# Scores of the later queries in steps of two chunks, with the keys' residues multiplied on 64 rows, in a two-block transformer kernel

## The chip, the cores and the metric

The kernel runs on one core of a Trainium2 chip. The metric is the device time of one launch in microseconds (us), from start to end; lower is better. TensorE (PE) multiplies matrices, VectorE (DVE), ScalarE (ACT) and GpSimd (POOL) do element-wise work, SyncE (SP) issues transfers. Each engine runs its own instructions in the order written; semaphores tie them together.

## What is computed

Two blocks over 1024 tokens of width 1024, in float32: first gated linear attention, a short convolution and a gated feed-forward layer; then spatial gating beside dilated attention. The change lies in the dilated attention alone (and in how GpSimd makes one residue). Cut to what matters:

```python
N_HEADS, HEAD_DIM, BLOCK = 16, 64, 128
DILATED_PATTERNS = ((128, 1), (512, 4), (2048, 16))

def dilated_pattern(q, k, v, slopes, window, dilation):
    ...
    s = jnp.einsum('bhrnqd,bhrnkd->bhrnqk', qb, kw) * (Dh ** -0.5)
    s = s - slopes[...] * (dist * dilation)
    s = jnp.where(valid[None, None, None], s, NEG_INF)
    m = jnp.max(s, axis=-1)
    p = jnp.exp(s - m[..., None])
    l = jnp.sum(p, axis=-1)
    o = jnp.einsum('bhrnqk,bhrnkd->bhrnqd', p, vw) / l[..., None]
    return o, m, l

def dilated_attention(q, k, v):
    outs = [dilated_pattern(qh, kh, vh, slopes, w, d) for (w, d) in DILATED_PATTERNS]
    m_all = max over the patterns of m
    alphas = [l * jnp.exp(m - m_all) for (_, m, l) in outs]
    return sum(a * o) / sum(alphas)
```

The kernel computes the three patterns at once: one dense causal score row per query, to which the penalty on the distance and the logarithm of the number of patterns that hold a key are added (a very negative number where there is none).

## The kernel before

**Split operands.** Every large product is made of three fast products. A float32 operand x becomes x_hi (a value rounded to the fast format) and the residue x_lo = x - x_hi, and W·x is W_hi·x_hi + W_hi·x_lo + W_lo·x_hi (L791 to L793). W_hi is made by ScalarE (L1185), W_lo by GpSimd in `split` (L686), one instruction of 1024 columns for each unit. A unit is one tile of 128 output columns of a weight: two halves of 512 tokens by 8 tiles of depth, that is 16 groups of three matmuls.

**Attention in stages.** Heads go in pairs; a pair has four units of projections (gates) left over from the input projection, and each of them is one *stage*: TensorE runs the unit's 16 groups of three dense matmuls, and behind each group stands a small piece of attention work. There are 32 stages (8 pairs by 4). Stage m of a pair scores head m // 2; with m even the early queries (tokens 0 to 511, an *even stage*), with m odd the later queries (512 to 1023, an *odd stage*), and beside it the softmax rows of the stage before are turned and multiplied with V. Which step stands behind which group is a string for each parity and engine: `PE_STEPS`, where a slash separates the groups, `ACT_STEPS` and `DVE_STEPS`, which are plain sequences. A step is skipped where it doesn't apply. The letters, with the lines:

- PE: s = scores of one chunk of keys (`score_chunk`, L1094 and L1095), t = four or fewer transposes of the softmax rows of the stage before (L1110), o = those with V (L1122, L1123), v = transposes of V (L1075, at the end of stage 0 of a pair only).
- ACT: e = exp of a query block (L1595), p = the fast part of a transposed chunk (L1605), w = W_hi of the next unit (L1185), a = a gate's tanh (L1618), q, k = the fast parts of the next head's queries and keys (L1460, L1464), O = half of the output (L1609), v = V's fast part (L1659), d, y = stores.
- DVE: r = scores plus bias with the running minimum (L2215), n = reciprocal and normalisation of a query block (L2225, L2227), l = residue of a transposed chunk (L2234), z = copy of the unit before out of PSUM (L2198), m = a gate's product (L2250), b = bias table of the next head (L2091, 1024 columns), q, k = residues of queries and keys (L2096, L2101), O = output (L2242), v = V's residue (L2281).

**Scores.** A head has 64 columns, and `att_q_split` uses all 128 rows: rows 0 to 63 hold q_hi and rows 64 to 127 hold q_lo, against the same keys loaded twice. One matmul with `att_k_hi` gives (q_hi + q_lo)·k_hi, a second with `att_k_lo` gives (q_hi + q_lo)·k_lo, into the same bank. An odd stage has four query blocks with two chunks of keys each: 512 and 128, 512 and 256, 512 and 384, 512 and 512 columns. They take turns in banks 2 and 0, and chunk n waits until DVE has taken chunk n - 2 (the semaphore `ttr`, L1090). Even stages have four chunks (128, 256, 384, 512), all in bank 2.

**What ties a stage to the next.** t0 of a stage waits for all four n of the stage before (`pn`, L1104), o waits for its l (`pl`, L1117), e for its block's last r, p for its t, l for its p, n for its e.

Of the kernel before, what the change touches and what calls it, by code (L numbers as in the profile page):

```python
# [25 lines left out]
P = 128  # L26
D = 1024
S = 1024
# [7 lines left out]
HEADS, DH = 16, 64  # L36
# [129 lines left out]
def steps_before(m):  # L166

    return 12 * (m // 2) + 4 * (m % 2)

def chunks_of(m):
# [16 lines left out]

PE_STEPS = [
    "t0/t1//o0 t2/s0/o1 t3/s1/o2 t4/s2/o3 t5/s3/o4 t6//o5 t7/o6/o7 v0 v1",  # L190
    "s0//s1/s2/t0/s3/s4/s5 o0 t1//s6/s7 o1 t2///o2 t3//o3",
]
PE_STEPS = [x.split("/") for x in PE_STEPS]
ACT_STEPS = [
# [2 lines left out]
]  # L197
DVE_STEPS = [
    "O l0 k l1 z l2 r0 l3 r1 n0 l4 r2 n1 l5 r3 n2 l6 m n3 l7",
    "v0 r0 v1 O r1 r2 z n0 l0 r3 r4 n1 l1 r5 m r6 r7 l2 n2 b l3 n3 q",  # L200
]

PE_REST = "t0 t1//o0 t2//o1 t3//o2 t4//o3 t5//o4 t6//o5 t7//o6//o7//".split("/")
# [26 lines left out]
def two_blocks(nc, xT, weights, vecs, gate_up, mix_w, mix_b, dist, logm, ident, out):  # L230
    f32, f32r = mybir.dt.float32, mybir.dt.float32r
    ALU = mybir.AluOpType
# [3 lines left out]
    with ctx:  # L236

        at = {}
# [45 lines left out]
        K2 = place("att_k", S, f32, xr + 4096)  # L284
        VT = place("att_v", S, f32, xr + 8192)
        QS = place("att_q_split", S, f32r, xr + 12288)
        KH = place("att_k_hi", S, f32r, xr + 16384)
        KL = place("att_k_lo", S, f32r, xr + 20480)
        VHL = place("att_v_split", [2, NBLK, P], f32r, xr + 24576)
# [393 lines left out]
        def _(pool):  # L683
            def split(u):
                pool.wait_ge(w_hi, u.count(1))
                pool.tensor_tensor(WL[:, u.slot], WR[:, u.slot], WH[:, u.slot].bitcast(f32),  # L686
                                   ALU.subtract).then_inc(w_lo, 1)

            def splits(c, n):
                if n >= 2:  # L690
# [79 lines left out]
        def _(pe):  # L770
# [308 lines left out]
            def score_chunk(pair, m, n):  # L1079

                i, c, w = chunks_of(m)[n]
                base, sb = steps_before(m), m % 2
                bank = 0 if sb and n % 2 else 2
                if n == 0 and sb == 0:
                    pe.wait_ge(q_lo, pair.count(2, m // 2 + 1))
                    pe.wait_ge(k_lo, pair.count(2, m // 2 + 1))
                if m == 1 and n == 1:
                    pe.wait_ge(v_lo, pair.count(2, 1))
                if n >= 1 + sb:
                    pe.wait_ge(ttr, pair.count(24, base + n - sb))  # L1090
                elif sb and n == 0:
                    pe.wait_ge(ttr, pair.count(24, base))
                dst = PA[:, bank, 0:w]
                pe.matmul(dst, QS[:, i * P:(i + 1) * P], KH[:, c:c + w], start=True, stop=False)  # L1094
                pe.matmul(dst, QS[:, i * P:(i + 1) * P], KL[:, c:c + w], start=False, stop=True  # L1095
                          ).then_inc(s_ready, 1)

            def turn_p(pair, m, k):

# [26 lines left out]
            def stage(pair, m, before=None, **have):  # L1126
                def between(g):
                    for kind, n in steps(PE_STEPS[m % 2][g], before=bool(before), first=m == 0):
                        if kind == "s":
                            score_chunk(pair, m, n)  # L1130
                        elif kind == "t":
                            turn_p(*before, n)
                        elif kind == "o":
                            weigh_v(*before, n)
                        else:
                            v_transposes(pair, n)
# [40 lines left out]
        def _(act):  # L1177
# [279 lines left out]

            def head_q(pair, h):
                act.wait_ge(q_in, pair.count(64, 32 * h + 32))
                act.activation(QS[:], Q2[:], ACT.Copy, scale=DH ** -0.5).then_inc(q_hi, 1)  # L1460

            def head_k(pair, h):
                act.wait_ge(k_in, pair.count(64, 32 * h + 32))
# [265 lines left out]
        def _(dve):  # L1729
# [363 lines left out]

            def head_q(pair, h):
                dve.wait_ge(q_hi, pair.count(2, h + 1))
                dve.scalar_tensor_tensor(QS[DH:P], Q2[DH:P], DH ** -0.5, QS[DH:P].bitcast(f32),  # L2096
                                         ALU.mult, ALU.subtract).then_inc(q_lo, 1)

            def head_k(pair, h):
# [323 lines left out]
```

## Time and profile before

| | us |
|---|---|
| three runs | 2412.66, 2410.06, 2413.32 |
| median | 2412.66 |
| profiled execution, its own time | 2410.62 |
| its span, first to last instruction | 2408.9 |
| TensorE busy in the span | 2351.6 |
| VectorE, ScalarE, GpSimd busy | 1345.0, 861.6, 736.6 |
| mean granted TensorE clock, share of full | 0.994 |

The span is 1.7 us shorter than the execution's own time. Rows name the line, the engine, the operation, the tiles (written <- read) and the shape; a time in brackets is how long the engine sat idle before, and who ended that. The end of a matmul is modelled, so its pace is read from starts: dense matmuls of 512 columns start 0.23 us apart although each is shown as 0.39 us long.

### The profile page before, as it was taken

Reading aid. Unit: us, or ns where it says so; the run is one execution under the profiler, and the core shown is the slowest. Engines: PE = TensorE matmul, PEld = TensorE weight load, DVE = VectorE, ACT = ScalarE, POOL = GpSimd, SP = SyncE. Lnnn points to the kernel's source line nnn. Section 1 sums busy time; section 2 is a strip of 40 time slices with the busy share of each in tenths; the row PEclk is TensorE's granted clock in tenths of the full one; section 3 lists DMA queues with packets and bytes.
Section 4 is the critical chain, followed back from the end, with each engine's and each line's share of the span. In section 5 each row is a group of like instructions: output and inputs, shape, how many; then the busy total and the mean of one; then the engine's idle time right before and its main releaser. Section 6 shows DMA issues by size and latency. Waiting matters only on the chain.

```text
span 2408.9 us, 29740 instructions
## 1 busy us (share of the span) xinstructions
PE 2351.6 (98%) x11076; PEld 1938.9 (80%) x11076; DVE 1345.0 (56%) x1790; ACT 861.6 (36%) x1293; POOL 736.6 (31%) x416
## 2 busy tenths in 40 slices
PE   9999999999999999999999999999999999999997
PEld 6888788878888888888888888778787787778886
DVE  4444763754444443347653444777877778753444
ACT  4422222242333331143343223555545555441122
POOL 2121221264555522222455555211122112212221
PEclk9999999999999999999999999999999999999998
DMA  3111222232222243233312223523233232353223
GB/s 133 44 44 35 88 79 96 86 144 85 79 79 80 84 169 105 70 114 114 118 53 83 101 95 111 178 76 113 78 113 106 77 113 78 105 181 124 105 96 113
DMA packets 69168, 237.94 MB, mean 99 GB/s; under 512 B 8241, under 2 KB 10449, under 8 KB 68945
## 3 DMA queue, kind: packets, MB, share of 16 engines
q1 hardware_dynamic: 53568, 181.53, 22.2%
q10 hardware_dynamic: 15504, 55.10, 5.7%
q8 instruction: 65, 1.06, 0.2%
q14 instruction: 31, 0.25, 0.0%
HBM read 177.35 MB, written 59.24 MB: 98 GB/s over the span
## 4 chain that ended last, share of the span: by engine, by line
PE 93%; DVE 4%; issue 1%; DMA 1%; ACT 1%; SPq 0%; DVEq 0%; ACTq 0%
PE dense L791 18%; PE dense L792 18%; PE dense L793 18%; PE dense L974 9%; PE dense L975 9%; PE dense L976 9%; PE aux L1110 3%; PE aux L1094 2%; PE aux L1095 1%; PE aux L1123 1%; PE aux L1122 1%; PE aux L1057 1%; DVE att_p_lo L2234 1%; DVE x_lo L1964 1%; PE aux L821 0%
## 5 line engine op out<-in xcount | busy, mean ns | idle before, releaser
L686 POOL TENSOR_TENSOR w_lo<-w_raw,w_hi 128x1024 fp32r<-128x1024 f32 x123 | 303.3, 2466 | 1097.0 <-ACT w_hi L1185 1087.9
L791 PE MATMUL dense<-x_hi,w_hi 128*128 128x512 f32 x1456 | 596.7, 410 | 5.8 <-DVE x_lo L1736 2.1
L792 PE MATMUL dense<-x_lo,w_hi 128*128 128x512 f32 x1456 | 570.7, 392 | 0.0
L793 PE MATMUL dense<-x_hi,w_lo 128*128 128x512 f32 x1456 | 570.7, 392 | 0.0
L1185 ACT CAST w_hi<-w_raw 128x1024 fp32r<-128x1024 f32 x121 | 127.1, 1050 | 555.7 <-PE dense L793 548.8
L793 PEld LDWEIGHTS dense<-x_hi,w_lo 128*128 128x128 f32 x1456 | 274.8, 189 | 59.8
L791 PEld LDWEIGHTS dense<-x_hi,w_hi 128*128 128x128 f32 x1456 | 275.5, 189 | 56.6 <-issue 8.6
L792 PEld LDWEIGHTS dense<-x_lo,w_hi 128*128 128x128 f32 x1456 | 276.1, 190 | 46.6 <-issue 1.9
L721 POOL TENSOR_TENSOR w_lo<-w_sums,w_hi 128x512 fp32r<-128x512 f32 x144 | 228.3, 1594 | 240.9 <-ACT w_hi L1341 240.9
L974 PE MATMUL dense<-x_hi,w_hi 128*128 128x512 f32 x576 | 226.1, 392 | 0.0
L976 PE MATMUL dense<-x_hi,w_lo 128*128 128x512 f32 x576 | 224.2, 389 | 0.0
L975 PE MATMUL dense<-x_lo,w_hi 128*128 128x512 f32 x576 | 224.2, 389 | 0.0
L1341 ACT CAST w_hi<-w_sums 128x512 fp32r<-128x512 f32 x144 | 89.2, 620 | 242.8 <-DVE w_sums L1973 176.1
L974 PE MATMUL dense<-x_sums_split,w_hi 128*128 128x512 f32 x432 | 168.4, 390 | 2.4 <-DVE work L2180 1.2
L976 PE MATMUL dense<-x_sums_split,w_lo 128*128 128x512 f32 x432 | 168.2, 389 | 0.0
L975 PE MATMUL dense<-x_sums_split,w_hi 128*128 128x512 f32 x432 | 168.1, 389 | 0.0
L1605 ACT CAST att_p_hi<-aux 128x512 fp32r<-128x512 f32 x192 | 92.2, 480 | 145.9 <-PE aux L1110 145.5
L2234 DVE TENSOR_TENSOR att_p_lo<-aux,att_p_hi 128x512 fp32r<-128x512 f32 x192 | 106.3, 554 | 60.3 <-ACT att_p_hi L1605 58.0
L791 PE MATMUL dense<-work_split,w_hi 128*128 128x512 f32 x352 | 137.0, 389 | 1.5 <-DVE work L2049 1.5
L793 PE MATMUL dense<-work_split,w_lo 128*128 128x512 f32 x352 | 136.9, 389 | 0.0
L792 PE MATMUL dense<-work_split,w_hi 128*128 128x512 f32 x352 | 136.9, 389 | 0.0
L974 PEld LDWEIGHTS dense<-x_hi,w_hi 128*128 128x128 f32 x576 | 108.2, 188 | 23.0 <-issue 1.0
(270 smaller groups left out, 3815.7 us busy)
## 6 DMA issues: line engine op xcount, KB each, us to landing
w_raw<-weights SPq DMA_DIRECT2D x163, 512.0 KB, 4.1
w_raw_b<-weights SPq DMA_DIRECT2D x34, 512.0 KB, 4.3
kept_qkv<-work ACTq DMA_DIRECT2D x24, 512.0 KB, 2.7
kept_m<-work ACTq DMA_DIRECT2D x22, 512.0 KB, 2.6
work<-kept_m SPq DMA_DIRECT2D x22, 512.0 KB, 3.3
residual<-xT SPq DMA_DIRECT2D x16, 512.0 KB, 7.1
kept_x<-residual ACTq DMA_DIRECT2D x16, 512.0 KB, 2.6
att_q<-kept_qkv SPq DMA_DIRECT2D x32, 256.0 KB, 3.9
```

Source lines behind the costliest of these rows:

```text
L686: pool.tensor_tensor(WL[:, u.slot], WR[:, u.slot], WH[:, u.slot].bitcast(f32), ALU.subtract).then_inc(w_lo, 1)
L721: pool.tensor_tensor(WL[:, h // 2, at4], quarter(p, i), WH[:, h // 2, at4].bitcast(f32), ALU.subtract).then_inc(*((d_lo, 1) if i < 6 else ...
L791: pe.matmul(dst, WH[:, u.slot, k], hi, start=(k == 0), stop=False)
L792: pe.matmul(dst, WH[:, u.slot, k], lo, start=False, stop=False)
L793: last = pe.matmul(dst, WL[:, u.slot, k], hi, start=False, stop=(k == nk - 1))
L974: pe.matmul(bank(b), wh, hi[:, j], start=(first and j == 0), stop=False, skip_group_check=True)
L975: pe.matmul(bank(b), wh, lo[:, j], start=False, stop=False, skip_group_check=True)
L976: last = pe.matmul(bank(b), wl, hi[:, j], start=False, stop=(j == 3), skip_group_check=True)
L1185: act.copy(WH[:, u.slot], WR[:, u.slot]).then_inc(w_hi, 1)
L1341: act.copy(WH[:, h // 2, 4 * (h % 2):4 * (h % 2) + 4], quarter(p, i)).then_inc(*((d_hi, 1) if i < 6 else (w_hi, 2)))
L1605: act.copy(PH[:, k % 2, lo:HALF], PA[:, bank, lo:HALF]).then_inc(ph, 1)
L2234: dve.tensor_tensor(PL[:, k % 2, lo:HALF], PA[:, bank, lo:HALF], PH[:, k % 2, lo:HALF].bitcast(f32), ALU.subtract).then_inc(pl, 1)
```

## The change

The strings of the odd stages on PE and DVE are new. On PE the eight s are replaced by four x, each for the two chunks of one query block (`score_chunks`); x waits until DVE has taken all chunks before it. x first multiplies both chunks with `att_k_hi` on 128 rows. Then it multiplies `att_k_lo` on 64 rows only, rows 0 to 63 for the first chunk and rows 64 to 127 for the second, with a new tile `att_q_hi_twice` that holds q_hi in both halves. The term q_lo·k_lo is left out in odd stages. ScalarE's q makes `att_q_hi_twice` (128 rows) and then rows 0 to 63 of `att_q_split`: two instructions of 1024 columns where one was. GpSimd's `split` becomes two instructions of 512 columns with one semaphore increment behind the second. Even stages keep their strings and `score_chunk`.

```diff
 PE_STEPS = [
     "t0/t1//o0 t2/s0/o1 t3/s1/o2 t4/s2/o3 t5/s3/o4 t6//o5 t7/o6/o7 v0 v1",
-    "s0//s1/s2/t0/s3/s4/s5 o0 t1//s6/s7 o1 t2///o2 t3//o3",
+    "//x0/t0//x1/o0 t1//x2/o1 t2//x3/o2 t3///o3",
 ]
 DVE_STEPS = [
     "O l0 k l1 z l2 r0 l3 r1 n0 l4 r2 n1 l5 r3 n2 l6 m n3 l7",
-    "v0 r0 v1 O r1 r2 z n0 l0 r3 r4 n1 l1 r5 m r6 r7 l2 n2 b l3 n3 q",
+    "v0 v1 O r0 r1 z l0 r2 r3 n0 l1 r4 r5 n1 l2 m r6 r7 n2 l3 b n3 q",
 ]
@@ def split (GpSimd)
-                pool.tensor_tensor(WL[:, u.slot], WR[:, u.slot], WH[:, u.slot].bitcast(f32),
-                                   ALU.subtract).then_inc(w_lo, 1)
+                for at4 in (slice(0, 4), slice(4, 8)):
+                    last = pool.tensor_tensor(WL[:, u.slot, at4], WR[:, u.slot, at4],
+                                              WH[:, u.slot, at4].bitcast(f32), ALU.subtract)
+                last.then_inc(w_lo, 1)
@@ new on TensorE
+            def score_chunks(pair, m, n):
+
+                pe.wait_ge(ttr, pair.count(24, steps_before(m) + 2 * n))
+                if m == 1 and n == 0:
+                    pe.wait_ge(v_lo, pair.count(2, 1))
+                both = chunks_of(m)[2 * n:2 * n + 2]
+                for (i, c, w), bank in zip(both, (2, 0)):
+                    pe.matmul(PA[:, bank, 0:w], QS[:, i * P:(i + 1) * P], KH[:, c:c + w], start=True, stop=False)
+                for (i, c, w), bank, rows in zip(both, (2, 0), (slice(0, DH), slice(DH, P))):
+                    pe.matmul(PA[:, bank, 0:w], QHH[rows, i * P:(i + 1) * P], KL[rows, c:c + w],
+                              start=False, stop=True).then_inc(s_ready, 1)
@@ head_q on ScalarE
-                act.activation(QS[:], Q2[:], ACT.Copy, scale=DH ** -0.5).then_inc(q_hi, 1)
+                act.activation(QHH[:], Q2[:], ACT.Copy, scale=DH ** -0.5)
+                act.activation(QS[0:DH], Q2[0:DH], ACT.Copy, scale=DH ** -0.5).then_inc(q_hi, 1)
@@ head_q on VectorE
-                dve.scalar_tensor_tensor(QS[DH:P], Q2[DH:P], DH ** -0.5, QS[DH:P].bitcast(f32),
+                dve.scalar_tensor_tensor(QS[DH:P], Q2[DH:P], DH ** -0.5, QHH[DH:P].bitcast(f32),
                                          ALU.mult, ALU.subtract).then_inc(q_lo, 1)
```

TensorE, the third query block of an odd stage. Before, its two chunks stand alone, behind groups 6 and 7 (the second is the one shown, with what follows it):

```order
L792 MATMUL dense<-x_lo,w_hi 128x512
L793 MATMUL dense<-x_hi,w_lo 128x512
L1090 REGISTER_ALU
L1094 MATMUL aux<-att_k_hi,att_q_split 128x384
L1095 MATMUL aux<-att_k_lo,att_q_split 128x384
L1119 REGISTER_ALU
L1122 MATMUL aux<-att_p_hi,att_v_split 128x512
```

Now both chunks stand behind group 8 as one x (the shape shown is that of the output):

```order
L795 MATMUL dense<-x_lo,w_hi 128x512
L796 MATMUL dense<-x_hi,w_lo 128x512
L1099 REGISTER_ALU
L1104 MATMUL aux<-att_k_hi,att_q_split 128x512
L1104 MATMUL aux<-att_k_hi,att_q_split 128x384
L1106 MATMUL aux<-att_k_lo,att_q_hi_twice 128x512
L1106 MATMUL aux<-att_k_lo,att_q_hi_twice 128x384
L794 MATMUL dense<-x_hi,w_hi 128x512
```

The last two chunks stood behind groups 9 and 10; their x3 stands behind group 11.

VectorE, from the middle of an odd stage. Before, n0 (L2227 on 640 columns) and l0 stand between the copy z and the third and fourth r:

```order
L2198 COPY work<-dense 128x1024
L2224 REGISTER_ALU
L2225 RECIPROCAL softmax_stats<-softmax_stats 128x1
L2227 TENSOR_SCALAR att_p_late<-att_p_late,softmax_stats 128x640
L2234 TENSOR_TENSOR att_p_lo<-aux,att_p_hi 128x512
L2212 REGISTER_ALU
L2215 ISA att_p_late,softmax_stats<-aux,att_bias,softmax_stats 128x256
```

Now the r of a block's two chunks stand together, and n0 behind the second block's:

```order
L2212 COPY work<-dense 128x1024
L2248 TENSOR_TENSOR att_p_lo<-aux,att_p_hi 128x512
L2226 REGISTER_ALU
L2229 ISA att_p_late,softmax_stats<-aux,att_bias 128x512
L2229 ISA softmax_stats 128x1
L2226 REGISTER_ALU
L2229 ISA att_p_late,softmax_stats<-aux,att_bias,softmax_stats 128x256
L2229 ISA softmax_stats 128x1
L2238 REGISTER_ALU
L2239 RECIPROCAL softmax_stats<-softmax_stats 128x1
L2241 TENSOR_SCALAR att_p_late<-att_p_late,softmax_stats 128x640
```

VectorE, the end of an odd stage. Before, the bias table b stands ahead of l3:

```order
L2227 TENSOR_SCALAR att_p_late<-att_p_late,softmax_stats 128x896
L2091 ISA
L2091 SCALAR_TENSOR_TENSOR att_bias<-distances,vectors,log_counts 128x1024
L2234 TENSOR_TENSOR att_p_lo<-aux,att_p_hi 128x128
L2224 REGISTER_ALU
L2225 RECIPROCAL softmax_stats<-softmax_stats 128x1
L2227 TENSOR_SCALAR att_p_late<-att_p_late,softmax_stats 128x1024
```

Now it stands behind l3 and ahead of n3:

```order
L2241 TENSOR_SCALAR att_p_late<-att_p_late,softmax_stats 128x896
L2248 TENSOR_TENSOR att_p_lo<-aux,att_p_hi 128x128
L2105 ISA
L2105 SCALAR_TENSOR_TENSOR att_bias<-distances,vectors,log_counts 128x1024
L2238 REGISTER_ALU
L2239 RECIPROCAL softmax_stats<-softmax_stats 128x1
L2241 TENSOR_SCALAR att_p_late<-att_p_late,softmax_stats 128x1024
```

## Rows read from the trace of the kernel before

**Rows 1.** The page, part 1: busy us, share of the span, instructions.

```profile
PE 2351.6 (98%) x11076; PEld 1938.9 (80%) x11076; DVE 1345.0 (56%) x1790; ACT 861.6 (36%) x1293; POOL 736.6 (31%) x416
```

**Rows 2.** Waits: engine, line, whom it waited for, us in total, times, longest.

```profile
PE aux L1094 <- DVE softmax_stats L2215: 25.1, 16, 1.9
```

**Rows 3.** Timeline (start, length in us), TensorE, the wait in two odd stages.

```profile
1807.44 0.39 PE L793 MATMUL dense<-x_hi,w_lo 128*128 128x512 f32 x1
1809.06 0.44 PE L1094 MATMUL aux<-att_k_hi,att_q_split 128*128 128x384 f32 x1 [1.23 <-DVE softmax_stats L2215]
1809.34 0.34 PE L1095 MATMUL aux<-att_k_lo,att_q_split 128*128 128x384 f32 x1
...
1844.66 0.39 PE L793 MATMUL dense<-x_hi,w_lo 128*128 128x512 f32 x1
1846.96 0.44 PE L1094 MATMUL aux<-att_k_hi,att_q_split 128*128 128x384 f32 x1 [1.91 <-DVE softmax_stats L2215]
```

**Rows 4.** Timeline ahead of the first wait, three engines; a half-length GpSimd residue elsewhere.

```profile
1806.07 1.93 DVE L2227 TENSOR_SCALAR att_p_late<-att_p_late,softmax_stats 128x640 f32<-128x640 f32 x1
1808.53 0.47 DVE L2215 CUSTOM_DVE_ANT_0 att_p_late<-aux,att_bias,softmax_stats 128x256 f32<-128x256 f32 x1
...
1805.26 2.39 POOL L686 TENSOR_TENSOR w_lo<-w_raw,w_hi 128x1024 fp32r<-128x1024 f32 x1 [16.91 <-ACT w_hi L1185]
...
1804.16 1.03 ACT L1185 CAST w_hi<-w_raw 128x1024 fp32r<-128x1024 f32 x1
...
1512.50 1.29 POOL L721 TENSOR_TENSOR w_lo<-w_sums,w_hi 128x512 fp32r<-128x512 f32 x1 [1.98 <-ACT w_hi L1341]
```

**Rows 5.** Timeline, TensorE: a run of 64-row matmuls, then part of it alone.

```profile
173.07 0.39 PE L793 MATMUL dense<-x_hi,w_lo 128*128 128x512 f32 x1
173.38 2.06 PE L918 MATMUL aux<-work 64*128 64x128 f32 x32
...
175.71 0.39 PE L792 MATMUL dense<-x_lo,w_hi 128*128 128x512 f32 x1
...
173.71 1.40 PE L918 MATMUL aux<-work 64*128 64x128 f32 x22
```

**Rows 6.** Timeline, TensorE: 32-row matmuls of 512 columns, then part of them alone.

```profile
56.54 0.39 PE L793 MATMUL dense<-x_hi,w_lo 128*128 128x512 f32 x1
...
60.82 0.39 PE L792 MATMUL dense<-x_lo,w_hi 128*128 128x512 f32 x1
...
57.39 2.30 PE L872 MATMUL aux<-work,gate_up_w 32*128 32x512 f32 x5
```

**Rows 7.** Timeline, TensorE: a chunk of 128 columns between dense matmuls.

```profile
1802.41 0.22 PE L1094 MATMUL aux<-att_k_hi,att_q_split 128*128 128x128 f32 x1
...
1802.87 0.39 PE L792 MATMUL dense<-x_lo,w_hi 128*128 128x512 f32 x1
```

**Rows 8.** Timeline, an odd stage's end: TensorE's last score, VectorE, ScalarE, TensorE.

```profile
1813.08 0.39 PE L1095 MATMUL aux<-att_k_lo,att_q_split 128*128 128x512 f32 x1
...
1813.66 0.75 DVE L2215 CUSTOM_DVE_ANT_0 att_p_late<-aux,att_bias,softmax_stats 128x512 f32<-128x512 f32 x1 [0.45 <-PE aux L1095]
...
1815.60 1.28 DVE L2091 SCALAR_TENSOR_TENSOR att_bias<-distances,vectors,log_counts 128x1024 f32<-128x1024 f32 x1
1816.80 0.28 DVE L2234 TENSOR_TENSOR att_p_lo<-aux,att_p_hi 128x128 fp32r<-128x128 f32 x1
...
1817.19 0.75 DVE L2227 TENSOR_SCALAR att_p_late<-att_p_late,softmax_stats 128x1024 f32<-128x1024 f32 x1
...
1814.45 1.15 ACT L1595 ACTIVATE att_p_late<-att_p_late,softmax_stats 128x1024 f32<-128x1024 f32 x1
...
1816.49 0.27 ACT L1605 CAST att_p_hi<-aux 128x128 fp32r<-128x128 f32 x1 [0.80 <-PE aux L1110]
...
1818.60 0.60 PE L1110 MATMUL aux<-identity,att_p_late 128*128 128x128 f32 x4
```

**Rows 9.** Window, length, busy us by engine, then granted clock: another such wait.

```profile
1764.00:1776.00 12.00, 10.10 (x43) 8.08 (x43) 9.96 (x20) 5.74 (x9) 4.74 (x2) 0.86 0.01 5
```

More of the change, by code:

```diff
@@ L286, in two_blocks @@
         QS = place("att_q_split", S, f32r, xr + 12288)
+        QHH = place("att_q_hi_twice", S, f32r, at["rstd"])
         KH = place("att_k_hi", S, f32r, xr + 16384)
@@ L1082, in score_chunk @@
                 base, sb = steps_before(m), m % 2
-                bank = 0 if sb and n % 2 else 2
-                if n == 0 and sb == 0:
+                bank = 2
+                if n == 0:
                     pe.wait_ge(q_lo, pair.count(2, m // 2 + 1))
                     pe.wait_ge(k_lo, pair.count(2, m // 2 + 1))
[L1087 to L1092, printed above, removed]
+                if n >= 1:
+                    pe.wait_ge(ttr, pair.count(24, base + n))
                 dst = PA[:, bank, 0:w]
@@ L1130, in between @@
                             score_chunk(pair, m, n)
+                        elif kind == "x":
+                            score_chunks(pair, m, n)
                         elif kind == "t":
```

## The prediction

> **What bounds the kernel now.** I read the page first: TensorE is busy 98% of the span [rows 1], so time goes only where TensorE does less work or waits less. Then the waits of TensorE: in the attention stages there is one large group, 16 waits of L1094 for VectorE's r, 25.1 us of idle time [rows 2]. Sixteen is one for each odd stage. The timeline shows what one costs: dense matmuls start 0.23 us apart, here L793 starts at 1807.44 and the next matmul at 1809.06, 1.39 us late, and L1095 follows 0.28 us behind instead of 0.17 (its weights were not loaded ahead), so 1.50 us. The stages with m = 1 lose more: 1844.66 to 1846.96 is 2.07 us late, 2.18 with the same 0.11 [rows 3]. Eight of each make 29.4 us. The cause is ahead of it on VectorE: n0 takes 1.93 us on 640 columns, while GpSimd's residue runs from 1805.26 to 1807.65, and r3, for which TensorE waits, starts only behind it [rows 4]; n3 on 1024 columns takes 0.75 [rows 8]. This is the wait that the change goes for.
>
> **TensorE's work in an x.** Two 64-row matmuls on different rows run as one: 22 of L918 with 128 columns take 1.40 us, the last of them started 0.27 before the end, so a pair takes 0.112 us [rows 5], while the same type of matmul with 512 columns takes 0.43 [rows 6], or 0.107 for 128: two for one. I use that for the residues. It saves the second chunk's L1095. A chunk of 128 columns cost 0.23 us for its two matmuls (1802.41 to 1802.87 less 0.23 for L791) [rows 7], and one narrow full-row matmul in the new place costs its width, 0.06: 0.17 saved. In the same way 256 saves 0.12, 384 saves 0.17, 512 saves 0.23. Together 0.70 us for an odd stage.
>
> But going from full rows to fewer and back is not free. From L793 at 173.07 to L792 at 175.71 are 2.64 us. Less 0.23 for L793, 0.23 for L791 and 16 pairs by 0.112, 0.39 remain for the way in and out [rows 5]. The 32-row run gives the same with 512 columns: 60.82 less 56.54 is 4.28, less 0.46 for two dense and 8 by 0.43, 0.40 [rows 6]. Bounds for one x: 0 (the chip could load the 64-row weights ahead here) and 0.40; I take 0.40, as both rows give it. Four x an odd stage are 1.6 less 0.70, **+0.88 us an odd stage, +14.1 us for 16.**
>
> **The old wait.** It goes. r0 to r5 now stand ahead of what needs them, x1 to x3 are three groups (2.05 us) and more apart, and VectorE's two r last at most 0.69 and 0.75 [rows 8]. n0 stands behind r3, and GpSimd's two halves of 1.29 [rows 4] follow the cast w. Whether VectorE slips in between them no longer matters to TensorE. The halves cost GpSimd 0.2 us a unit, behind which nothing waits: w_lo is due a whole unit (18 us) later. -29.4 us.
>
> The Trainium skill (SBUF — State Buffer, Terms) says that VectorE and GpSimd share a port pair under an exclusive lock, held for a full instruction; n0's 1.93 us [rows 4] agrees, and a half-length instruction would by it hold VectorE up half as long.
>
> **What is late next.** I lay the new order out from the start of an odd stage, a group of three dense matmuls at 0.68 us.
> First, o0. x0 stands behind three groups: its residues start at 2.54, r0 starts 0.58 after them (the latency of 1813.08 to 1813.66 [rows 8]), r0 and r1 end at 4.1, since both are now needed for e0. Then ScalarE's e0 (0.83), w (1.03 [rows 4]) and p0 (0.59), the two others by the width of e3 [rows 8], VectorE's l0 (0.69), and o0 can start at 7.3. TensorE comes to it at 7.14 (seven groups, x0, t0, x1). A wait of 0.2, and 0.11 for weights not loaded ahead: 0.31.
> Second, the end. x3 stands behind group 11, where the last two chunks stood behind groups 9 and 10. The chain from the start of x3 to the next stage's t0, in which each step needs the one before: full-row matmuls 0.46, the switch 0.20, 0.58 to r6, r6 0.62, r7 0.75, e3 1.19, p3 0.27, l3 0.31, then b, which now stands between l3 and n3, 1.21, the reciprocal 0.20, n3 0.75, the semaphore 0.06 [rows 8]; 6.60, and 6.49 with VectorE's instructions overlapping by 0.07 here and there. TensorE has between the same points: x3 1.09, five groups 3.41, o2, t3 and o3 0.61: 5.1. So it is 1.4 us early in all, of which 0.2 to 0.3 pass at o3 for l3 and the rest at t0 for n3, and with the 0.11 behind t0 it loses 1.5. Before, r7 had begun 0.58 behind a score that came 1.2 us earlier in the stage, and b ran in an idle gap ahead of l3: n3 ended at 1817.94, t0 started at 1818.60 [rows 8], 0.66 us to spare. In stages with m = 1 the gate product m stands ahead of r6 and makes it 0.5 us later: 2.0.
> Waits after: 0.31 + 1.5 in eight stages and 0.31 + 2.0 in eight, 33 us; the last odd stage has no b, -1.2: **31.7 us against 29.4 before, +2.3.**
>
> The extra instruction in ScalarE's q (about 1.1 us, e3's length for as many columns [rows 8]) stands at the end of an odd stage. Behind it are O, p0 and k, then VectorE's k, for which s0 waits; laid out in the same way, k is done 1.1 us before s0 is due, so it costs nothing, and up to 1 us a stage if that cover is gone. Dropped q_lo·k_lo costs nothing.
>
> **Clock.** In 1764 to 1776, around one such wait, the granted clock was 0.86 of full [rows 9], that is, a part of it at 1.2 GHz. The waits that follow one another at o3 and t0 are about as long, so I leave this as it is; two such windows go or come at some 1.7 us each.
>
> **Sum.** 2410.6 (the profiled execution) + 14.1 - 29.4 + 31.7 = 2427.0. The median lies 2 us above that execution; half of this added gives **2428 us, 0.6% slower**.
>
> **Rivals.**
> 1. *Faster: n3 comes in time.* Place: the chain from x3 to t0. It decides at 1.4 us: if that chain is 5.1 us or less instead of 6.5, there is no wait at the end, and only o0's 0.31 is left, 4.9 us in all. The time would be 2410.6 + 14.1 - 29.4 + 4.9 = 2400, and 2397 with the two slow-clock windows gone. For it: TensorE had 0.66 us to spare [rows 8]. Against it: each length in the chain is a row, and b alone takes 1.28 of VectorE. Chance 0.13.
> 2. *The switch is free.* Then TensorE has 25 us less work, but it comes sooner to o0 and o3, where the chains over ScalarE are as long as before. Laid out anew, o0 waits 0.6 us longer and o3 0.2 to 0.6, so only about 10 us come back: 2418. Against it are both rows of the switch. Chance 0.12.
> 3. *The residues run one after another*, so that the change doesn't do what it says. 0.58 us more work an odd stage, almost all inside the waits for o0 and o3, which shrink by as much: 2430. Rows 5 speak against it. Chance 0.06.
> 4. *More waits:* k or the first score of an even stage is late by some 0.5 us, and slow-clock windows behind the waits: 2438. Chance 0.08.
> 5. *The end's wait is half of what I think* (0.7 us a stage): 2417. Chance 0.09.
> My forecast has 0.52.
>
> **How the numbers follow.** A measurement of this kernel tells 0.2% (4.8 us) from no change: 2407.8 to 2417.5 is the same. Faster is rival 1, 0.13. Same are halves of rivals 2 and 5, 0.11. The rest is slower, 0.76. The range leaves out rival 1 and the upper half of rival 4: 2410 to 2437.
>
> **What would show it.** L1094's wait for VectorE in odd stages gone; in its place waits of L1110 (t0) and of the last L1122 in odd stages for VectorE, near 1.1 us 15 times and 0.2 to 0.7 us 16 times; n0 near 0.6 to 1.1 us instead of 1.93 and more. Starts 0.2 us apart more than the width before and behind each pair of 64-row matmuls, the two of a pair starting together. Odd stages as long as now, even stages 1.2 us longer. I am wrong if t0 starts straight behind its group, or if the matmul behind an x starts 0.23 us after the residues.

## The result, and the profile after

| | before | after |
|---|---|---|
| median | 2412.99 us (2410.06 to 2414.69, 4 runs) | 2439.9 us (2435.22 to 2440.96, 4 runs) |
| after over before | | 1.0109, 95% interval 1.0092 to 1.0127 |
| profiled execution, its own time | 2410.62 | 2440.96 |
| its span | 2408.9 | 2439.2 |
| mean granted clock | 0.994 | 0.993 |

The change costs 27 us, 1.1%. The forecast was 15 us, with a range that ended at 2437.

The page of the profile after, part 1, answers [rows 1]: TensorE works 25 us longer, VectorE 48 us less.

```profile
PE 2376.4 (97%) x11076; PEld 1927.4 (79%) x11076; DVE 1296.8 (53%) x1790; ACT 870.7 (36%) x1309; POOL 794.8 (33%) x539
```

The waits of TensorE for VectorE in the attention stages. The one of [rows 2] is gone, and two stand in its place, 32 at o and 16 at t0 (the end of a matmul is modelled, so these totals are too small; below I read the lateness from starts):

```profile
PE aux L1133 <- DVE att_p_lo L2248: 20.2, 32, 1.2
PE aux L1121 <- DVE att_p_late L2241: 10.6, 16, 0.9
```

The timeline of TensorE in one odd stage (m = 3), from x0 to o0, with one group in between left out:

```profile
1816.38 0.39 PE L796 MATMUL dense<-x_hi,w_lo 128*128 128x512 f32 x1
1816.61 0.45 PE L1104 MATMUL aux<-att_k_hi,att_q_split 128*128 128x512 f32 x2
1816.99 0.50 PE L1106 MATMUL aux<-att_k_lo,att_q_hi_twice 64*128 64x512 f32 x2
1817.42 0.50 PE L794 MATMUL dense<-x_hi,w_hi 128*128 128x512 f32 x1
1817.76 0.40 PE L795 MATMUL dense<-x_lo,w_hi 128*128 128x512 f32 x1
...
1821.48 0.40 PE L796 MATMUL dense<-x_hi,w_lo 128*128 128x512 f32 x1
1822.37 0.50 PE L1133 MATMUL aux<-att_p_hi,att_v_split 128*128 128x512 f32 x1 [0.50 <-DVE att_p_lo L2248]
...
1828.33 0.62 PE L1104 MATMUL aux<-att_k_hi,att_q_split 128*128 128x512 f32 x2
1828.88 0.50 PE L1106 MATMUL aux<-att_k_lo,att_q_hi_twice 64*128 64x512 f32 x2
1829.31 0.50 PE L794 MATMUL dense<-x_hi,w_hi 128*128 128x512 f32 x1
```

A row with x2 holds both chunks. The two residues of x0 (512 and 128 columns) take 0.43 us to the next start, and so do the two of x3 (512 and 512): the narrower one costs nothing beside the wider. That is the two for one of [rows 5]. The way in and out is in the same rows: from x0 at 1816.61 to L795 at 1817.76 are 1.15 us, less 0.23 for L794, less 0.29 for 640 full-row columns, less 0.23 for the residues, leaves 0.40 us. The same sum for x3, with L795 0.34 behind L794, is 1.32 - 0.23 - 0.46 - 0.23 = 0.40.

o0 should have followed L796 at 1821.71 and starts at 1822.37, 0.66 us late. The same view at the end of this stage, then at the end of a stage with m = 1:

```profile
1832.31 0.40 PE L796 MATMUL dense<-x_hi,w_lo 128*128 128x512 f32 x1
1833.11 0.33 PE L1133 MATMUL aux<-att_p_hi,att_v_split 128*128 128x128 f32 x1 [0.40 <-DVE att_p_lo L2248]
...
1833.89 0.39 PE L796 MATMUL dense<-x_hi,w_lo 128*128 128x512 f32 x1
1835.16 0.66 PE L1121 MATMUL aux<-identity,att_p_late 128*128 128x128 f32 x4 [0.88 <-DVE att_p_late L2241]
...
1871.49 0.40 PE L796 MATMUL dense<-x_hi,w_lo 128*128 128x512 f32 x1
1873.07 0.33 PE L1133 MATMUL aux<-att_p_hi,att_v_split 128*128 128x128 f32 x1 [1.19 <-DVE att_p_lo L2248]
...
1874.31 0.39 PE L796 MATMUL dense<-x_hi,w_lo 128*128 128x512 f32 x1
1875.13 0.66 PE L1121 MATMUL aux<-identity,att_p_late 128*128 128x128 f32 x4 [0.43 <-DVE att_p_late L2241]
```

Here o3 is 0.57 us late and t0 1.04; with m = 1 they are 1.35 and 0.59 late. Each wait costs about another 0.11 behind it: from o0 to the next start are 0.34 us (1822.37 to 1822.71) instead of 0.23, as in the prediction. So a stage loses 0.77 at o0, and 1.83 (m = 3) or 2.16 (m = 1) at its end: 16 by 0.77, 8 by 1.83 and 8 by 2.16 are 44 us, where the forecast had 31.7.

VectorE in the same stage: the two r of x0, then of x3, and what follows up to n3, for which t0 waits; then ScalarE's three steps ahead of o0.

```profile
1817.68 0.69 DVE L2229 CUSTOM_DVE_ANT_0 att_p_late<-aux,att_bias 128x512 f32<-128x512 f32 x1 [1.67 <-PE aux L1106]
1818.29 0.08 DVE L2229 DVE_READ_ACCUMULATOR2_ANT softmax_stats<- 128x1 f32 x1
1818.65 0.35 DVE L2229 CUSTOM_DVE_ANT_0 att_p_late<-aux,att_bias,softmax_stats 128x128 f32<-128x128 f32 x1 [0.28 <-DVE softmax_stats L2229]
...
1829.57 0.69 DVE L2229 CUSTOM_DVE_ANT_0 att_p_late<-aux,att_bias 128x512 f32<-128x512 f32 x1 [0.26 <-PE aux L1106]
...
1830.54 0.75 DVE L2229 CUSTOM_DVE_ANT_0 att_p_late<-aux,att_bias,softmax_stats 128x512 f32<-128x512 f32 x1 [0.28 <-DVE softmax_stats L2229]
...
1832.97 1.28 DVE L2105 SCALAR_TENSOR_TENSOR att_bias<-distances,vectors,log_counts 128x1024 f32<-128x1024 f32 x1
...
1834.35 0.75 DVE L2241 TENSOR_SCALAR att_p_late<-att_p_late,softmax_stats 128x1024 f32<-128x1024 f32 x1
```

```profile
1819.05 0.83 ACT L1609 ACTIVATE att_p_late<-att_p_late,softmax_stats 128x640 f32<-128x640 f32 x1 [3.76 <-DVE softmax_stats L2229]
...
1819.87 1.03 ACT L1198 CAST w_hi<-w_raw 128x1024 fp32r<-128x1024 f32 x1
1820.93 0.59 ACT L1619 CAST att_p_hi<-aux 128x512 fp32r<-128x512 f32 x1
```

The second r starts 0.97 us after the first, and VectorE sits idle for 0.28 of it, released by its own earlier result. The chain was laid out with 0.62.

The group of instructions that held up TensorE before, n0, is short now (columns: busy us, mean ns of one): 554 ns each, against 1.93 us in [rows 4].

```profile
L2241 DVE TENSOR_SCALAR att_p_late<-att_p_late,softmax_stats 128x640 f32<-128x640 f32 x16 | 8.9, 554 | 0.6
```

The lengths of the stages, from the last dense matmul of one unit to that of the next, read from the starts in the timelines; sums are over the four stages of a pair:

| us | m = 2 | m = 3 | m = 0 | m = 1 | sum |
|---|---|---|---|---|---|
| before | 19.04 | 17.99 | 18.36 | 19.53 | 74.92 |
| after | 20.90 | 18.20 | 20.12 | 19.07 | 78.29 |

The row "before" is one pair; its stages with m = 2 scatter from 18.4 to 19.0 us (the reason stands under e7_switch_alone). Eight pairs by 3.37 us are 27 us, all of the difference of the medians; over all stages but the first the difference is 26.8 us. (The profiled executions differ by 30 us; the rest lies outside the attention.) Both traces have two stages in the attention with a stretch at a lower granted clock, so the clock is no part of it; the window that answers [rows 9]:

```profile
1716.00:1728.00 12.00, 11.56 (x57) 9.43 (x56) 8.86 (x17) 6.15 (x11) 2.53 (x2) 0.86 0.64 171
```

### The profile page after: what moved, and what is told of

Same layout as the page of the kernel before. It is cut to its first block, busy times and chain, and to the rows that moved or that the text cites. A ratio compares the mean times of both kernels' runs of the same rounds, so it can differ in the third digit from the quotient of the medians.

```text
span 2439.2 us, 29866 instructions
## 1 busy us (share of the span) xinstructions
PE 2376.4 (97%) x11076; PEld 1927.4 (79%) x11076; DVE 1296.8 (53%) x1790; ACT 870.7 (36%) x1309; POOL 794.8 (33%) x539
## 4 chain that ended last, share of the span: by engine, by line
PE 84%; DVE 6%; issue 4%; ACT 2%; POOL 1%; DMA 1%; ACTq 0%; DVEq 0%; SPq 0%; POOLq 0%
PE dense L794 16%; PE dense L796 16%; PE dense L795 16%; PE dense L977 8%; PE dense L979 8%; PE dense L978 8%; PE aux L1121 2%; PE aux L1133 1%; PE aux L1134 1%; DVE att_p_late L2229 1%; POOL att_mixed L754 1%; DVE att_bias L2105 1%; PE aux L1106 1%; DVE att_p_lo L2248 1%; ACT w_hi L1198 1%
## 5 line engine op out<-in xcount | busy, mean ns | idle before, releaser
L688 POOL TENSOR_TENSOR w_lo<-w_raw,w_hi 128x512 fp32r<-128x512 f32 x246 | 366.1, 1509 | 1068.1 <-ACT w_hi L1198 1058.9
L794 PE MATMUL dense<-x_hi,w_hi 128*128 128x512 f32 x1456 | 603.6, 415 | 5.5 <-POOL w_lo L688 2.1
L796 PE MATMUL dense<-x_hi,w_lo 128*128 128x512 f32 x1456 | 572.2, 393 | 0.0
L795 PE MATMUL dense<-x_lo,w_hi 128*128 128x512 f32 x1456 | 571.4, 392 | 0.0
L794 PEld LDWEIGHTS dense<-x_hi,w_hi 128*128 128x128 f32 x1456 | 275.7, 189 | 70.9 <-issue 23.2
L796 PEld LDWEIGHTS dense<-x_hi,w_lo 128*128 128x128 f32 x1456 | 275.0, 189 | 59.8
L795 PEld LDWEIGHTS dense<-x_lo,w_hi 128*128 128x128 f32 x1456 | 276.5, 190 | 45.9 <-issue 2.0
L794 PE MATMUL dense<-work_split,w_hi 128*128 128x512 f32 x352 | 137.1, 390 | 1.7 <-DVE work L2063 1.7
L796 PE MATMUL dense<-work_split,w_lo 128*128 128x512 f32 x352 | 137.0, 389 | 0.0
L795 PE MATMUL dense<-work_split,w_hi 128*128 128x512 f32 x352 | 137.0, 389 | 0.0
L1951 DVE TENSOR_TENSOR residual<-dense,residual 128x1024 f32<-128x1024 f32 x32 | 39.2, 1225 | 169.3 <-PE dense L796 169.3
```

The source lines that it names most:

```text
L688: last = pool.tensor_tensor(WL[:, u.slot, at4], WR[:, u.slot, at4], WH[:, u.slot, at4].bitcast(f32), ALU.subtract)
L794: pe.matmul(dst, WH[:, u.slot, k], hi, start=(k == 0), stop=False)
L795: pe.matmul(dst, WH[:, u.slot, k], lo, start=False, stop=False)
L796: last = pe.matmul(dst, WL[:, u.slot, k], hi, start=False, stop=(k == nk - 1))
```

## The experiments

The first theory was that of the forecast, with one correction: r behind r costs 0.97 us instead of 0.62, because the second waits for the first one's result, and this stands twice on TensorE's path in an odd stage (ahead of o0, and ahead of t0). Its rivals were that the end's chain was misread (b, the residues' latency), that the 64-row matmuls cost more than 0.40, and that GpSimd's halves hold something up. The kernels take the change apart from both sides: parts of it added to the kernel before, and parts of it undone in the changed kernel.

### What the old wait was worth: halves and order apart

e1_halves is the kernel before with GpSimd's residue in halves only.

```diff
-                pool.tensor_tensor(WL[:, u.slot], WR[:, u.slot], WH[:, u.slot].bitcast(f32),
-                                   ALU.subtract).then_inc(w_lo, 1)
+                for at4 in (slice(0, 4), slice(4, 8)):
+                    last = pool.tensor_tensor(WL[:, u.slot, at4], WR[:, u.slot, at4],
+                                              WH[:, u.slot, at4].bitcast(f32), ALU.subtract)
+                last.then_inc(w_lo, 1)
```

> The kernel before with GpSimd's residue in two instructions of 512 columns and nothing else. Theory A (the waits come from the order on VectorE and from what holds n0 up): n0 is held up only until the end of the first half, some 1.1 us less, in all 16 odd stages; L1094 waits 0.4 to 0.9 us instead of 1.5 to 2.2: 2413 - 18 = 2395 us. Rival (VectorE doesn't get in between the halves): n0 as long as before, 2413 us, or 1 us more.

Measured: 2394.53 us, ratio 0.9925 (0.9908 to 0.9941). All 16 waits are shorter. The view shows only the eight with m = 1; those with m = 3 have fallen below what it counts, but by the starts they are still 0.28 us late, and their stages (16.87 us) are 0.37 longer than without any wait (16.50, next run), those with m = 1 (18.43) 1.07:

```profile
PE aux L1096 <- DVE softmax_stats L2217: 6.1, 8, 0.8
```

n0 takes 1.15 us on average here instead of 2.27, which fits the reading that a second instruction of 512 columns gives VectorE an opening in the middle.

e2_halves_n0_later has the halves, and n0 behind the fifth r (r4):

```diff
-    "v0 r0 v1 O r1 r2 z n0 l0 r3 r4 n1 l1 r5 m r6 r7 l2 n2 b l3 n3 q",
+    "v0 r0 v1 O r1 r2 z l0 r3 r4 n0 n1 l1 r5 m r6 r7 l2 n2 b l3 n3 q",
```

> As e1_halves, and in the odd stages' order on VectorE n0 stands behind the third and fourth r (... z l0 r3 r4 n0 n1 ...); TensorE's steps are those of before. Theory A: no wait of TensorE is left in odd stages: 2413 - 28 = 2385 us. Rival (what is late next comes at once, at o0 or o3): 2395 us or more.

Measured: 2380.69 us, ratio 0.9865 (0.9849 to 0.9882). TensorE has no wait for VectorE left in an odd stage. Stages: 18.99, 16.50, 18.34, 17.36.

e6_n0_later has only that string; GpSimd's residue is whole, as before.

> The kernel before with only the order on VectorE of e2_halves_n0_later; GpSimd's residue in one piece. Theory A (the wait is made by what stands behind n0): TensorE doesn't wait in odd stages, as in e2: 2381 to 2383 us. Rival (the halves are needed as well): 2390 us or more.

Measured: 2380.67 us, ratio 0.9876 (0.986 to 0.9893), and the same stages within 0.03 us. So once n0 is out of the way of r3, the halves are worth nothing, and the string alone brings 31 us. Against before, a stage with m = 3 is 1.49 us shorter and one with m = 1 2.17, where the forecast read 1.50 and 2.18 for the old wait, 29.4 us in all. The two stretches at a lower clock, some 1.6 us each, are gone as well.

e9_whole_residue is the mirror: the changed kernel with GpSimd's residue in one instruction again (the diff of e1_halves the other way round).

> The changed kernel with GpSimd's residue in one piece as before. In the new order n0 stands behind r3 and starts 2.7 us after GpSimd in the stages with m = 3, so it is held up for little of it. Forecast's view (the halves do nothing once n0 stands later): 2440 us, within 3 us. Rival (VectorE's other instructions with two operands are held up too): 2445 us or more.

Measured: 2440.48 us, ratio 1.0114 (1.0097 to 1.0132), as the changed kernel. The halves neither help nor harm there. The forecast had them at nothing.

### The switch by itself

e7_switch_alone is e2_halves_n0_later with the residue of each second chunk on 64 rows, without a partner:

```diff
-                pe.matmul(dst, QS[:, i * P:(i + 1) * P], KL[:, c:c + w], start=False, stop=True
+                rows = slice(0, DH) if sb and n % 2 else slice(0, P)
+                pe.matmul(dst, QS[rows, i * P:(i + 1) * P], KL[rows, c:c + w], start=False, stop=True
```

> As e2_halves_n0_later (no waits of TensorE in the attention stages), but in odd stages the residue product of each second chunk (four a stage, 64 in all) is multiplied on rows 0 to 63 of att_q_split alone, which leaves out q_lo times k_lo there; nothing is paired. It measures the switch of rows by itself. Forecast's value, 0.40 us each: 2381 + 25 = 2406 us. Rival (free): 2381 us. Rival (half hidden): 2393 us.

Measured: 2403.53 us (10 runs), 22.8 us over e2_halves_n0_later, or 0.36 us for each of the 64. The odd stages are longer by 1.50 and 1.51 us, four by 0.375; the stage with m = 2 is shorter by 0.42. That is a hold of TensorE at its start, which e2_halves_n0_later has in six of eight such stages and e7_switch_alone in none: from the last dense matmul of m = 1 over o3 to the first of the next unit are 1.01 us (from 1838.30) in the one and 0.56 (from 1849.74) in the other:

```profile
1839.31 0.49 PE L793 MATMUL dense<-x_hi,w_hi 128*128 128x512 f32 x1 [0.23 <-issue]
```

```profile
1850.30 0.49 PE L793 MATMUL dense<-x_hi,w_hi 128*128 128x512 f32 x1
```

No release that the profile shows ends it, and its cause stays open. Four of the eight stages with m = 2 before have it and six in the changed kernel, so it is hardly part of what the change costs. The price of a switch is therefore read from the odd stages. TensorE around one such residue of 384 columns:

```profile
1803.45 0.34 PE L1096 MATMUL aux<-att_k_hi,att_q_split 128*128 128x384 f32 x1
1803.72 0.44 PE L1098 MATMUL aux<-att_k_lo,att_q_split 64*128 64x384 f32 x1
1804.08 0.50 PE L1125 MATMUL aux<-att_p_hi,att_v_split 128*128 128x512 f32 x1
1804.42 0.40 PE L1126 MATMUL aux<-att_p_lo,att_v_split 128*128 128x512 f32 x1
```

By widths these three intervals would be 0.17, 0.17 and 0.23; they are 0.27, 0.36 and 0.34, that is 0.10, 0.19 and 0.11 more, 0.40 together. The Trainium skill (TensorEngine Tiling (Array Packing), Key Properties) says that a change of mode drains TensorE and gives no price; these rows agree, and the price here is 0.36 to 0.40 us for the way in and out together.

e3_full_rows is the changed kernel with the residues on all 128 rows, in the same steps of two chunks:

```diff
-                for (i, c, w), bank, rows in zip(both, (2, 0), (slice(0, DH), slice(DH, P))):
-                    pe.matmul(PA[:, bank, 0:w], QHH[rows, i * P:(i + 1) * P], KL[rows, c:c + w],
+                for (i, c, w), bank in zip(both, (2, 0)):
+                    pe.matmul(PA[:, bank, 0:w], QS[:, i * P:(i + 1) * P], KL[:, c:c + w],
                               start=False, stop=True).then_inc(s_ready, 1)
```

> The changed kernel, steps of two chunks and all orders kept, but the keys' residues are multiplied on 128 rows with att_q_split as before. Takes away the switch of rows (0.40 us an x as forecast) and adds back 0.58 us of matmuls an odd stage: 1.0 us less work an odd stage. Theory A: TensorE then comes sooner to o0 and o3 and waits there; half is eaten: 2440 - 8 = 2432 us. Rival B (the loss is mostly the switch): 2440 - 16 = 2424 us or less. Rival C (the switch costs nothing and only the pairing saved): 2449 us.

Measured: 2438.84 us, ratio 1.0106 (1.0089 to 1.0123). The expectation missed, by 7 us. The work did become less: stages of m = 3, 0 and 1 are 17.64, 20.11 and 18.53, and those of m = 2 22.35 with, 21.15 without a stretch at a lower clock. Without such stretches a pair is 0.86 us shorter than in the changed kernel, 6.9 us in all, near the 8 of theory A; o0 is 1.02 us late instead of 0.66, so TensorE waits for part of what it saves. The clock takes the rest back. The mean granted clock is 0.988 instead of 0.993, and seven of the stages with m = 2 have a stretch at a lower clock, where the changed kernel has two. Windows of the same place, the changed kernel first, then e3_full_rows (columns: length, busy us of PE, PEld, DVE, ACT, POOL, granted clock):

```profile
1792.00:1804.00 12.00, 10.15 (x53) 7.78 (x53) 10.60 (x17) 7.96 (x13) 4.45 (x3) 1.00 0.40 132
```

```profile
1790.00:1802.00 12.00, 10.12 (x44) 7.60 (x44) 10.99 (x19) 7.53 (x11) 4.41 (x3) 0.86 0.35 120
```

0.86 over 12 us means that a part of them ran at 1.2 GHz and the rest at 2.4. Such a stage is some 1.2 us longer here and 1.4 to 1.5 in the changed kernel, so seven against two take back nearly 6 of the 6.9 us. What TensorE did before the fall is the wait ahead of it: o3 starts 1.6 us late in these stages, 1.35 us in the changed kernel.

```profile
1793.03 0.33 PE L1133 MATMUL aux<-att_p_hi,att_v_split 128*128 128x128 f32 x1 [1.43 <-DVE att_p_lo L2248]
```

That wait does not decide it: the last stage with m = 2 has the same 1.6 us and no fall. Why there are five more falls stays open. The number of them changes from one trace to the next with edits that have nothing to do with it (two in e5_r_apart, three in e9_whole_residue, four in e10_own_wait_second).

### The end's chain, and r behind r

e4_b_last is the changed kernel with b behind n3:

```diff
-    "v0 v1 O r0 r1 z l0 r2 r3 n0 l1 r4 r5 n1 l2 m r6 r7 n2 l3 b n3 q",
+    "v0 v1 O r0 r1 z l0 r2 r3 n0 l1 r4 r5 n1 l2 m r6 r7 n2 l3 n3 b q",
```

> The changed kernel with the bias table b behind n3 instead of ahead of it (... l3 n3 b q). Theory A: t0 of even stages no longer waits for n3 (1.0 and 0.6 us), o0 of even stages waits some 0.5 us instead since everything behind b on VectorE is as late: 2440 - 9 = 2431 us. Rival B (the waits are not the order's): 2440 us.

Measured: 2433.19 us, ratio 1.0084 (1.0067 to 1.0102). The waits of t0 are gone, but there are more at o, since q and all behind it now come later by as much:

```profile
PE aux L1133 <- DVE att_p_lo L2248: 25.7, 41, 1.2
```

Of the 10.6 us at t0 about 3.5 are gained (a pair's stages sum to 77.85), and 3 more as no stage of the attention has a stretch at a lower clock. So b ahead of n3 explains the wait at t0, but it is not the 12 us that the forecast lacks: b was priced at 1.21 us in the chain and takes 1.19 there (1832.97 to the reciprocal at 1834.16).

e5_r_apart is the changed kernel in which the second r doesn't wait for the first:

```diff
-                if c:
-                    dve.wait_ge(ttr, pair.count(24, base + n))
                 dve.wait_ge(s_ready, pair.count(24, base + n + 1))
...
-                    scale=-1.0, scalar=(STAT[:, 0, b:b + 1] if c else 3.0e38), op0=ALU.add, op1=ALU.min,
+                    scale=-1.0, scalar=3.0e38, op0=ALU.add, op1=ALU.min,
```

> The changed kernel, in which the r of a block's second chunk starts its minimum anew and doesn't wait for the first chunk's r (it leaves out that the block's maximum takes in both chunks, so the softmax is scaled by another number). Theory D (r directly behind r costs 0.97 us instead of 0.62, since the second waits for what the first has written; this is the term that was too small): l0, l3 and n3 come 0.35 us sooner, TensorE waits 0.7 us less an odd stage: 2440 - 11 = 2429 us, o0's lateness 0.3 instead of 0.67 us. Rival (the gap between the two r is the unpaired finish of TensorE's two matmuls): nothing changes, 2440 us.

Measured: 2428.21 us, ratio 1.007 (1.0053 to 1.0087); 11.7 us less than the changed kernel by the medians, 14.3 by the stages without a stretch at a lower clock, 9 by the two ratios. The edit does a little more than take the wait away: the second r no longer reads the first one's minimum and is 0.69 us long instead of 0.75. The r of x3, 0.62 us apart as the forecast had them:

```profile
1820.88 0.69 DVE L2227 CUSTOM_DVE_ANT_0 att_p_late<-aux,att_bias 128x512 f32<-128x512 f32 x1 [0.65 <-PE aux L1106]
1821.50 0.08 DVE L2227 DVE_READ_ACCUMULATOR2_ANT softmax_stats<- 128x1 f32 x1
1821.50 0.69 DVE L2227 CUSTOM_DVE_ANT_0 att_p_late<-aux,att_bias 128x512 f32<-128x512 f32 x1
```

And o0, whose wait was 0.66 us, is 0.24 late (L796 at 1813.22, then o0 at 1813.69); the forecast had 0.2. At the end the gain falls at o3 (0.17 late instead of 0.57, with m = 1 0.86 instead of 1.35), and t0 is as late as in the changed kernel.

```profile
1813.22 0.40 PE L796 MATMUL dense<-x_hi,w_lo 128*128 128x512 f32 x1
1813.69 0.49 PE L1133 MATMUL aux<-att_p_hi,att_v_split 128*128 128x512 f32 x1
```

e8_r_apart_b_last has both edits, to see whether they share a path.

> The changed kernel with the edits of e5_r_apart and of e4_b_last together (leaves out the same). If waits at different places only add, 2440 - 11 - 7 = 2422 us; if the one hides the other, 2427 us or more. In either case it stays above 2413 us, since the work of the switches (14 us net) is left and o0 and o3 still wait.

Measured: 2418.82 us, ratio 1.0032 (1.0017 to 1.0046): 21.1 us less than the changed kernel, against 11.7 and 6.7 for each alone. They add up: by the stages without a stretch at a lower clock it is 18.2 us against 14.3 and 3.5, and no stage has such a stretch here, while e5_r_apart has two. Even so it is 38 us slower than e6_n0_later: the switch of 64 x and what is left of the waits stay.

e10_own_wait_second asks what the 0.28 us are. In the changed kernel r waits first for its own earlier result, then for the scores; here the two are exchanged.

```diff
-                if c:
-                    dve.wait_ge(ttr, pair.count(24, base + n))
                 dve.wait_ge(s_ready, pair.count(24, base + n + 1))
+                if c:
+                    dve.wait_ge(ttr, pair.count(24, base + n))
                 dve.sem_inc(turns, 1)
```

> The changed kernel with one edit: VectorE's r waits for the scores first and for its own earlier result second (before: the other way round). In the changed kernel the second r of a block starts 0.97 us after the first and VectorE sits idle 0.28 us ahead of it. Theory A: the 0.28 us is what the wait for its own result takes, wherever it stands; the gap stays at 0.28 us and the median at 2440 (2437 to 2442). Theory B: a good part of it is the work of VectorE's sequencer on what stands behind that wait (the second wait and a semaphore step); with one wait fewer behind it the gap falls to 0.15 to 0.2 us, and the median by 16 odd stages x 2 places on TensorE's path x 0.1 = 3 us, to 2437. Theory C: the gap goes altogether, 2430.

Measured: 2438.25 us, ratio 1.0113 (1.0096 to 1.013). The interval doesn't part this from the changed kernel, but the trace does: the gap is 0.17 us instead of 0.28, in every block, and it is no longer put down to a release but to issue.

```profile
1825.74 0.69 DVE L2229 CUSTOM_DVE_ANT_0 att_p_late<-aux,att_bias 128x512 f32<-128x512 f32 x1 [0.33 <-PE aux L1106]
1826.36 0.08 DVE L2229 DVE_READ_ACCUMULATOR2_ANT softmax_stats<- 128x1 f32 x1
1826.62 0.75 DVE L2229 CUSTOM_DVE_ANT_0 att_p_late<-aux,att_bias,softmax_stats 128x512 f32<-128x512 f32 x1 [0.17 <-issue]
```

A pair's stages sum to 77.8 us instead of 78.3, 4 us in all, of which two more stages with a stretch at a lower clock (22.2 and 22.4 us long instead of 20.7) take 3 back. So the order of the two waits is worth 0.11 of the 0.28 us, as theory B has it.
## Why the prediction was wrong

**What held.** The direction, and nearly every step.
- *Old wait gone, -29.4.* -31 by e6_n0_later, a change of one string; 1.49 and 2.17 us a stage where 1.50 and 2.18 were read.
- *Two for one.* Both residues in 0.43 us, the same for 128 and for 512 columns of the second. Rival 3 is out.
- *The switch, 0.40 an x.* 0.40 by the starts, 0.36 to 0.375 by e7_switch_alone. Rival 2 is out: x0 takes 0.92 us and x3 1.09, as laid out. (1.6 less 0.70 is 0.90 and not 0.88, so the term should have read +14.4. Less the wait at o0, an odd stage is 0.93 us longer than in e6_n0_later, 15 us in all.) By luck the way from x3 to r6 came out at the forecast's 1.24: the residues start 0.11 sooner than laid out and r6 follows them 0.69 us behind, not 0.58.
- *The places of the new waits.* o0, o3 and t0 and no others; t0 16 times. The first rival, n3 in time, is out.
- *b.* 1.19 us in the chain where 1.21 was said. Moved behind n3 (e4_b_last) it gives 3.5 us by the stages; 3 more of the 6.7 are the clock. *The halves* cost nothing (e9_whole_residue). *The extra instruction of q* draws no wait at s0 and costs nothing.
- *Even stages longer, odd ones as before,* in kind: +0.21 and -0.46 us for the odd. The even ones grew by 1.86 and 1.76, half as much again as the 1.2 that was said.

**The step that failed** is a term of the walk under "What is late next": "r6 0.62, r7 0.75", and in the same way "r0 and r1 end at 4.1". I priced the first r of a block by the distance at which two r follow each other when the second needs nothing of the first. With x they stand together and the second needs the first one's result. It measured 0.97, so +0.35 us, once ahead of o0 and once ahead of t0. Against the rows: from x3 at 1828.33 to t0 at 1835.16 are 6.83 us, and the forecast had 6.49; TensorE's 5.1 beside it was right, and so were the 1.24 from x3 to r6 (1829.57). From x0 at 1816.61 to o0 at 1822.37 are 5.76 us where the forecast had 5.25 (0.35 for r behind r, 0.16 in small pieces, 0.12 of them on the way from e0 to o0). 16 stages by twice 0.35 are 11.2 us. The waits are 44 us instead of 31.7: 7.4 of the 12.5 more are at o0 (16 by 0.77 instead of 0.31) and 4 at the stages' ends, and the 1.2 us that were booked for the missing b of the last odd stage are not in this count. e5_r_apart, in which that one step is as I had priced it, takes 2428.2 us. That this is the forecast's 2428 to the last digit is partly luck, since its edit takes 9 to 14 us away depending on how it is read.

One more size was off, and hidden. With m = 1 the product m makes r6 0.79 us later (x3 at 1867.51, r6 at 1869.54, that is 2.03 us instead of 1.24), where 0.5 was said. The end of such a stage still costs 2.16 us and not 2.6, because TensorE is itself 0.40 us later there, by the hold described under e7_switch_alone.

The trace of before did show this price, in stages that I had not laid out. [Rows 8] are from a stage with m = 3, where r7 waits for TensorE (0.45 us idle) and its own wait is over by then; the 0.62 is the distance without any wait. With m = 1, the product m holds r6 up, TensorE's score is ready, and r7 waits for r6 alone. Six of the eight stages with m = 1 have this, five of them with the 0.97 us and the 0.28 idle of the changed kernel. Among the waits of before, and in the timeline of one such stage:

```profile
DVE att_p_late L2215 <- DVE softmax_stats L2215: 1.6, 6, 0.3
```

```profile
1851.07 0.68 DVE L2215 CUSTOM_DVE_ANT_0 att_p_late<-aux,att_bias 128x512 f32<-128x512 f32 x1
...
1852.03 0.75 DVE L2215 CUSTOM_DVE_ANT_0 att_p_late<-aux,att_bias,softmax_stats 128x512 f32<-128x512 f32 x1 [0.28 <-DVE softmax_stats L2215]
```

There TensorE waited for nothing behind it, so it cost nothing. The change puts the second r directly behind the first in all four blocks and both kinds of odd stage (64 waits, 17.2 us of VectorE's time), twice a stage on TensorE's path.

**Why the range missed too.** I widened it by rivals that were each a whole mechanism (switch free, n3 in time), and left the lengths in the walk without an error of their own. The chain has some ten links; it is passed 32 times, so 0.1 us in one link that stands in both walks is 3 us. Nearly all of the way to 2440 is one link that was off by 0.35. Rival 4 ("more waits", 2438) came nearest in time, but for another reason: k and the first score of the even stages drew no wait, and no stretch at a lower clock was added (two before, two after).

**Where the gain went.** The change removes 29 us of waiting that one moved n0 would remove alone. The steps of two chunks put both r of a block, which stood 1.0 to 4.7 us apart, and whose own wait cost TensorE nothing, in a row behind a later start of TensorE, and put 64 switches of 0.40 us on TensorE, where the saved residues return 0.70 us in a stage. Against e6_n0_later the changed kernel is 59 us slower: some 15 for the work of x, and 44 for waits that are not in e6_n0_later at all.

**The better version.** e6_n0_later, the kernel before with n0 moved behind r4 on VectorE, takes 2380.7 us: 0.9876 (0.986 to 0.9893) of the kernel before.

## What to carry to other kernels

When a change moves two dependent instructions of an engine together, look for the wait that used to be over by the time it was reached, and don't price the pair by rows in which the two are independent. Look for the pair in every kind of stage, and among the waits of the engines that are not the bottleneck: here the row with the true price was in the trace of before. Where one instruction is late behind a slow one that nobody needs soon, move the slow one first: here one step in one string was worth more than the whole change. A step that changes the number of rows on TensorE must save more than its way in and out, so gather many matmuls behind one such change instead of making it for each pair.

## What was unexpected of the hardware

- An r that waits for the one before starts 0.28 us after its end, and 0.11 of that goes when the second wait in the instruction stream stands ahead of the wait for its own result (0.17 us then, e10_own_wait_second). A reciprocal and the n that waits for it are only 0.03 us apart, so it is not the price of every such wait:

```profile
1831.22 0.16 DVE L2239 RECIPROCAL softmax_stats<-softmax_stats 128x1 f32<-128x1 f32 x1
1831.41 0.69 DVE L2241 TENSOR_SCALAR att_p_late<-att_p_late,softmax_stats 128x896 f32<-128x896 f32 x1
```

- n0 of 640 columns: 2.27 us on average before, 1.15 with GpSimd's halves, 0.55 moved behind the r. The Trainium skill (SBUF — State Buffer, Terms) has VectorE and GpSimd take turns at one port pair, each for a full instruction; the three numbers agree.
- A kernel with less work on TensorE had more stretches at 1.2 GHz: seven in e3_full_rows against two in the changed kernel, for nearly 6 us. That the one brings the other isn't shown.
